# Value stage of a retrieval layer: 768 gathered and 1280 dense columns, and one weight split per two blocks

## The reference, cut to what matters

```python
def peer_layer(x, wq, keys, U, Vt):
    ...
    idx = jnp.take_along_axis(...)                       # 128 experts of 16384 for each token
    gate = jax.nn.softmax(best, axis=-1).astype(x.dtype)
    def blk(args):
        xb, ib, gb = args
        u = U[ib]
        hid = jax.nn.gelu(jnp.einsum('td,thkd->thk', xb, u))
        v = Vt[ib]
        return jnp.einsum('thk,thkd->td', gb * hid, v)   # the value stage
...
x = x + peer_layer(h2, ...)
return rms_norm(x, norm_f_g)
```

## Time and profile before

| | |
|---|---|
| median of 3 runs | 1992.54 us |
| the profiled execution | 1993.4 us |
| its span in the profile | 1991.7 us |
| value stage, first to last v_lo | 1504.37 to 1974.63 us |
| busy in the span: PE, DVE, ACT, POOL | 70%, 81%, 44%, 51% |
| TensorE's granted clock in the value stage | 1.00 (2.4 GHz) |

### The profile page before, as it was taken

The page is one execution under the profiler, slowest core; times in us unless marked ns, Lnnn a source line. Parts: engine busy times, 40 slices in busy tenths (PEclk is TensorE's granted clock), DMA queues, the critical chain, the costliest instruction groups (busy, mean ns, idle before and its releaser), DMA issues.

```text
span 1991.7 us, 22500 instructions
## 1 busy us (share of the span) xinstructions
PE 1401.3 (70%) x7813; PEld 1229.1 (62%) x7813; DVE 1614.4 (81%) x2065; ACT 875.9 (44%) x1279; POOL 1009.1 (51%) x705
## 2 busy tenths in 40 slices
PE   6999999999999999900000002221369999999997
PEld 6988998888888889900000001121257888888886
DVE  6466785556755566899999999987988999999998
ACT  4354443454444444322222235577754444444444
POOL 4002320000000003488888888888888768887772
PEclk9999999999999999955555555555579999999999
DMA  6555444545655555999999999999957999999996
GB/s 213 187 187 196 153 165 145 167 165 172 207 190 182 200 185 184 365 419 414 420 417 419 410 400 419 422 414 418 417 196 283 400 374 398 400 404 392 377 381 230
DMA packets 145660, 601.81 MB, mean 302 GB/s; under 512 B 14720, under 2 KB 14736, under 8 KB 110096
## 3 DMA queue, kind: packets, MB, share of 16 engines
q0 software_dynamic: 58048, 364.41, 45.2%
q1 hardware_dynamic: 87504, 236.02, 33.7%
HBM read 598.29 MB, written 2.10 MB: 301 GB/s over the span
## 4 chain that ended last, share of the span: by engine, by line
PE 61%; issue 14%; DVE 11%; POOL 6%; DMA 6%; ACT 1%; SPq 0%; DVEq 0%; POOLq 0%; ACTq 0%
PE acc L1956 8%; PE acc L1957 8%; PE acc L1958 8%; DVE slots L1632 6%; POOL slots L614 6%; PE acc L1937 5%; PE acc L1939 5%; PE acc L1940 5%; PE acc L2268 3%; PE acc L2269 3%; PE acc L2270 3%; PE scr L2269 3%; PE scr L2268 3%; PE scr L2270 3%; DMA slots<-in_peer_u,expert 3%
## 5 line engine op out<-in xcount | busy, mean ns | idle before, releaser
L1088 DVE TENSOR_TENSOR w_lo<-raw,w_hi 128x1024 fp32r<-128x1024 f32 x266 | 328.8, 1259 | 204.1 <-ACT w_hi L698 201.2
L1632 DVE SCALAR_TENSOR_TENSOR slots<-slots,acc 128x2048 f32<-128x2048 f32 x184 | 415.5, 2285 | 34.8 <-DMA slots<-in_peer_u,expert 32.8
L698 ACT ACTIVATE w_hi<-raw 128x1024 fp32r<-128x1024 f32 x272 | 281.9, 1056 | 360.3 <-PE acc L1958 176.4
L650 POOL DMA_INDIRECT starts<-in_v_gather,expert x256 | 357.8, 1398 | 102.8 <-DVE X L1856 73.0
L614 POOL DMA_INDIRECT slots<-in_peer_u,expert x256 | 257.8, 1007 | 100.2 <-issue 59.0
L624 POOL TENSOR_TENSOR slots<-slots,N 128x2048 f32<-128x2048 f32 x61 | 276.1, 4527 | 34.0 <-DMA slots<-in_peer_u,expert 33.9
L1022 ACT ACTIVATE v_hi<-v_raw 128x1344 fp32r<-128x1344 f32 x128 | 170.5, 1332 | 262.4 <-PE scr L2270 182.6
L938 ACT ACTIVATE slots<-slots 128x2048 f32<-128x2048 f32 x61 | 116.5, 1910 | 334.1 <-POOL slots L624 334.1
L2225 PE MATMUL scr<-hot_a,hot_b 128*128 128x128 f32 x448 | 89.0, 369 | 220.6 <-DVE hot_b L1709 158.3
L1856 DVE SCALAR_TENSOR_TENSOR X<-starts,weight,X 128x704 f32<-128x704 f32 x256 | 242.1, 946 | 1.4 <-issue 0.9
L1956 PE MATMUL acc<-w_hi,hT_hi 128*128 128x512 f32 x576 | 225.7, 392 | 0.6 <-DVE w_lo L1088 0.6
(11 more groups left out here) (329 smaller groups left out, 3079.6 us busy)
## 6 DMA issues: line engine op xcount, KB each, us to landing
raw<-in_w_in SPq DMA_DIRECT2D x88, 1024.0 KB
v_raw<-in_v_dense SPq DMA_DIRECT2D x128, 672.0 KB
raw<-in_w_o SPq DMA_DIRECT2D x16, 1024.0 KB
raw<-in_peer_wq SPq DMA_DIRECT2D x16, 1024.0 KB
raw<-in_w_a_up SPq DMA_DIRECT2D x8, 1024.0 KB
raw<-in_w_b_up SPq DMA_DIRECT2D x8, 1024.0 KB
slots<-in_peer_u,expert POOLq DMA_INDIRECT x256, 8.9
starts<-in_v_gather,expert POOLq DMA_INDIRECT x256
```

Of the source, the lines that this page charges most:

```text
L650: pool.indirect_dma_start(starts[j][:, :], None, v_gather[:, :], bass.IndirectOffsetOnAxis(ap=expert[:, s // NSEL, s % NSEL:s % NSEL + 1], ...
L698: a.activation(w_hi[:, m % 2, k, :], raw[:, m % 2, k, :], ACT.Copy).then_inc(hi_ready, 1)
L1088: v.tensor_tensor(w_lo[:, m % 2, k, :], raw[:, m % 2, k, :], w_hi[:, m % 2, k, :].bitcast(fp32), ALU.subtract).then_inc(lo_ready, 1)
L1632: v.scalar_tensor_tensor(out=slots[j][:, :], in0=slots[j][:, :], scalar=1.0, in1=row, op0=ALU.mult, op1=ALU.mult, accum_out=hid_sum[:, t, ...
```

## The change

CW goes from 704 to 768, so each gathered row is 64 columns wider and the dense part 64 columns narrower (1280; PE's third piece has 256 columns). The buffers of the value stage get new places in SBUF.

The weight splits of both tiles become one operation of 512 columns on ACT and one on DVE, in odd blocks only. For that the dense weights of both tiles are seen as rows of 8 KiB of one tensor, `weight_rows`, at the same addresses as before; `both_weights` takes one piece of two of its rows, the lower address first. Which of the two halves belongs to which tile is told by `side_of`.

```diff
-CW = 704
+CW = 768
...
 def weights_at(n):
     pair = (n + 1) // 2
-    return [(pair, 1 - n % 2)] if 0 < n and pair < BLOCKS // 2 else []
+    return [pair] if n % 2 and pair < BLOCKS // 2 else []
+
+def side_of(n, t):
+    return t if n < P // PIECES else 1 - t
...
+        def both_weights(pair):
+            q, at0 = 2 * pair // (P // PIECES), 2 * pair % (P // PIECES)
+            rows = sorted(((0, 14, 16, 19)[q] + at0 // 16, 2 + 2 * q + at0 // 16))
+            cols = slice(at0 % 16 * P, (at0 % 16 + 2) * P)
+            return weight_rows[:, rows[0]:rows[1] + 1:rows[1] - rows[0], cols]
...
-            def high_e(pair, t):
+            def high_e(pair):
                 if pair >= 2:
                     act.wait_ge(v_used, 4 * pair - 4)
-                q, at0 = 2 * pair // (P // PIECES), 2 * pair % (P // PIECES)
-                a.activation(e_hi[:, pair % 2, t, :],
-                             weight_of[t][q][:, at0:at0 + 2, :].rearrange("p a s -> p (a s)"), ACT.Copy
-                             ).then_inc(e_hi_ready, 1)
+                a.activation(e_hi[:, pair % 2, :, :], both_weights(pair), ACT.Copy).then_inc(e_hi_ready, 1)
...
-            def low_e(pair, t):
-                dve.wait_ge(e_hi_ready, 2 * pair + t + 1)
-                q, at0 = 2 * pair // (P // PIECES), 2 * pair % (P // PIECES)
-                v.tensor_tensor(e_lo[:, pair % 2, t, :],
-                                weight_of[t][q][:, at0:at0 + 2, :].rearrange("p a s -> p (a s)"),
-                                e_hi[:, pair % 2, t, :].bitcast(fp32), ALU.subtract).then_inc(e_ready, 1)
+            def low_e(pair):
+                dve.wait_ge(e_hi_ready, pair + 1)
+                v.tensor_tensor(e_lo[:, pair % 2, :, :], both_weights(pair), e_hi[:, pair % 2, :, :].bitcast(fp32),
+                                ALU.subtract).then_inc(e_ready, 2)
...
                 if n == 0:
-                    low_e(0, 0)
-                    low_e(0, 1)
+                    low_e(0)
                 add_start(2 * n)
-                for pair, t in weights_at(n):
-                    low_e(pair, t)
+                for pair in weights_at(n):
+                    low_e(pair)
                 add_start(2 * n + 1)
...
-                    pe.wait_ge(e_ready, n // 2 * 2 + t + 1)
+                    pe.wait_ge(e_ready, n // 2 * 2 + 2)
```

More of the change, by code:

```diff
@@ L310, in build @@
         masks_t = at("masks_t", 144, [MASKED, P])
-        weight_of1 = at("weight_of1", 32, [P, P])
-        weight_of = [[at(f"weight_of0_{q}", kib, [P // PIECES, P]) for q, kib in enumerate((16, 128, 144, 168))],
+        weight_rows = at("weight_rows", 16, [21, 16 * P])
+        weight_of1 = weight_rows[:, 2:10, :].rearrange("p r (a s) -> p (r a) s", s=P)
+        weight_of = [[weight_rows[:, r:r + 2, :].rearrange("p r (a s) -> p (r a) s", s=P) for r in (0, 14, 16, 19)],
                      [weight_of1[:, q * P // PIECES:(q + 1) * P // PIECES, :] for q in range(PIECES)]]
-        v_raw = [at(f"v_raw{n}", kib, [DW]) for n, kib in enumerate((112, 117.25, 2.75))]
+        def both_weights(pair):
[3 more added lines that the diff above has]
+            return weight_rows[:, rows[0]:rows[1] + 1:rows[1] - rows[0], cols]
+        v_raw = [at(f"v_raw{n}", kib, [DW]) for n, kib in enumerate((112, 117, 3))]
         v_hi = at("v_hi", 184, [2, DW], f32r)
-        v_lo = [at(f"v_lo{n}", kib, [DW], f32r) for n, kib in enumerate((160, 10.75))]
+        v_lo = [at(f"v_lo{n}", kib, [DW], f32r) for n, kib in enumerate((160, 11))]
         e_hi, e_lo = at("e_hi", 97, [2, NT, 2 * P], f32r), at("e_lo", 101, [2, NT, 2 * P], f32r)
@@ L321, in build @@
         y_first = at("y_first", 128, [NT, CW])
-        y_dense = at("y_dense", 133.5, [NT, DW])
+        y_dense = at("y_dense", 134, [NT, DW])
         starts = [at(f"starts{n}", kib, [CW]) for n, kib in enumerate(
-            (194.5, 197.25, 122.5, 125.25, 165.25, 105, 107.75, 24, 26.75, 29.5, 32.25, 35, 37.75, 40.5))]
+            (194, 197, 122, 125, 165, 105, 108, 24, 27, 30, 33, 36, 39, 42))]
         ff_room = at("ff_room", 200, [2 * KB])
@@ L1041, in square_first @@
                              ).then_inc(squared, 1)
-            high_e(0, 0)
-            high_e(0, 1)
+            high_e(0)
             for n in range(BLOCKS):
@@ L1047, in _ @@
                     high_v(n)
-                for pair, t in weights_at(n):
-                    high_e(pair, t)
+                for pair in weights_at(n):
+                    high_e(pair)
                 if n == FIRST_FROM:
@@ L2260, in add @@
                 def add(t, pieces, low):
-                    pe.wait_ge(e_ready, n // 2 * 2 + t + 1)
+                    pe.wait_ge(e_ready, n // 2 * 2 + 2)
                     flat = (acc, scr)[t][:, :, :].rearrange("p a n -> p (a n)")
-                    eh, el = e_hi[:, n // 2 % 2, t, e_cols], e_lo[:, n // 2 % 2, t, e_cols]
+                    eh, el = e_hi[:, n // 2 % 2, side_of(n, t), e_cols], e_lo[:, n // 2 % 2, side_of(n, t), e_cols]
                     for at0, end in pieces:
```

## The result

The changed kernel takes 1997.03 us (median of 16 runs, 1992.29 to 2001.60), the kernel before, run beside it, 1990.86 us (16 runs, 1987.39 to 1995.50). The ratio is 1.0030, 95% interval 1.0022 to 1.0037: slower by 6.2 us on the medians, where +7.3 was forecast. The profiled execution took 1996.16 us, with a span of 1994.4. Its value stage, from the first v_lo at 1503.73 to the last at 1977.60, is 473.9 us long against 470.3 before: +3.6 in these two executions.

The account below looks back on a forecast made before the run. PE bounds the value stage before the change at 3.64 us a block, DVE after it at 3.665. 465.9 undisturbed plus 11.7 late is 477.6 against 470.3, +7.3 on 1992.54: 1999.8 us, range 1991.2 to 2007.5.

Parts of the forecast that it names:

- DVE becomes the bound, alternating: Value stage: DVE sets the step, 3.46 us in even and 3.87 in odd blocks, mean 3.665, above PE's 3.48.
- The price of the dependence: In even blocks the second addition waits for the first, both writing X: 0.20 us that the split used to hide.
- 1.13 + 0.93: Part of DVE's even block of 3.46 us: 1.13 between the two additions' starts, then 0.93 to the next v_lo.
- Late loads: Dense loads landing late for v_hi in the value stage: 11.7 us forecast, between 0 and 20, against 7.5 before.
- 12 x 0.35: Growth in late loads: some 12 events, each with some 0.35 us less room, added to 7.5 for 11.7 us.
- rival 1: Value stage: late loads hidden, PE having 0.18 us a block to spare; with 3 us late, 1991.2 us; chance 0.28.
- the forecast's 8.4 to 16: Main case for the value stage: DVE the bound, with 8.4 to 16 us of lateness; chance 0.50.
- The sum: Value stage 465.9 us undisturbed plus 11.7 late, 477.6 against 470.3: +7.3 us, the run 1999.8 us.
- POOL: "waits for DVE's additions, as now": POOL in the value stage: as many gathers as before, waiting for DVE's additions as before; no size given.
- Rivals 2 and 3: 2: dependence costs DVE nothing, even block 3.26, 1987.3 us, chance 0.06; 3: DMA bounds, 2003.3 us, 0.16 with lateness above 16.

Follow-up runs that it names:

- two_tiles: The changed kernel with additions alternating between the two tiles, and tile 0's square and gain moved to the end: 2010.73 us, ratio 1.0103 to the kernel before.
- half_rows: The changed kernel with gathered rows of half the length (384 columns), each read twice by the addition: 1990.94 us, ratio 0.9998 to the kernel before.

## Why the prediction was right

- *DVE becomes the bound, alternating.* Right. Forecast 3.46 and 3.87, measured 3.52 and 3.86; PE's side waits 26.6 + 3.8 us on v_lo, against 8.0 + 3.7 before, where some 23 against 3.7 was forecast; the split takes 0.679 us (0.69).
- *The price of the dependence.* Forecast 0.20, from the pairs of the earlier trace rows. The runs show 2.13 - 1.94 = 0.19 without gathers, and 2.19 - 1.94 = 0.25 with them. The step that was mis-sized is "1.13 + 0.93", which took the pair of the earlier trace rows to the new width by the slope of DVE alone. That gives about what the pair takes without POOL (2.15 forecast, 2.13 measured); at the new width POOL's next issue starts 0.09 us into the second addition, which then takes 1.08 in place of 1.02, and 63 x 0.06 = 3.8 us were missed (the odd blocks, 0.01 shorter than forecast, give 0.6 back). So undisturbed the stage is 469.0, not 465.9. The rule of the Trainium skill in VectorE: DVE Perf Modes, The DRAIN you can't avoid, by which the wait would cost nothing, disagrees with two_tiles: 1.94 against 2.13 for the same two additions.
- *Late loads.* Forecast 11.7, from "12 x 0.35" on top of before's 7.5; measured 4.9. Of that, DVE idled 1.7 us ahead of a late v_lo (2.4 in its row, 0.7 of it before the first block) and some 2.4 for gathers (2.7 in their row, 0.3 of it the dependence), and the gain multiplication took 0.9; five pairs shorter than 2.19 give 0.4 back. So some 2 us is loads. This step failed: v_hi did wait for loads more often, 65 times for 147.2 us against 36 times for 77.5, but few of these waits reached DVE. The count was misread too: the 36 waits do not come in threes, in the trace they stand in 21 groups, most of them of one or two blocks. And the prediction counted each event of waits on ACT as lost time on DVE, with no cover behind it. But ACT starts v_hi as soon as the load is there, and since DVE itself is the bound, v_hi was mostly ready before DVE came to it (v_hi after such a wait runs from 1565.81 to 1567.09, and v_lo starts at 1567.54). To that extent rival 1 was right: 4.9 us lies in its range, below 8.4, and not in the forecast's 8.4 to 16. Whether the loads themselves landed later at 2.3% more bytes is not shown.
- *The sum.* The two errors, +3.1 undisturbed and -6.8 late, partly cancel (-3.7 on the stage): 473.9 against 477.6 for the stage in the profiled execution, which is +3.6 where +7.3 was forecast. On the medians it is +6.2 against +7.3, and that they are so close is in part luck: undisturbed the stage grew by 469.0 - 462.7 = 6.3 where 3.2 was forecast, and lateness, for which 4.2 more was forecast, did not grow in the two traced executions (7.6 and 4.9).
- *POOL: "waits for DVE's additions, as now".* The answer held for the time, but it wasn't priced. POOL's issues filled 354.2 us of the stage before and fill 382.0 now, with at least 0.30 between each two; the next thing that makes DVE faster at this width, two_tiles, ran into them at once.
- *Rivals 2 and 3* fall by two_tiles and half_rows.

## What to carry to other kernels

Removing an instruction that stands between two dependent ones can cost more than the instruction did: price the gap it filled, on the engine that will be the bound after the change, and look at what the other engines start at the moment in which the second of the two comes due. Two changes to one stage must be priced together, since the first may move the bound onto what the second lengthens. An engine's wait counts only as far as the engine that sets the step waits too.

## What the runs showed of the hardware that was not expected

POOL's issue of an indirect transfer of 128 rows takes longer beside a busy DVE, and can draw an instruction of DVE out in turn. It takes 0.94 to 2.96 us beside a busy DVE, a mean of 1630 ns in two_tiles; while DVE idles there for lack of a gather, from 1519.79 to 1522.16, it takes 0.94 or 0.95:

```profile
1521.23 0.94 POOL L663 DMA_INDIRECT starts<-in_v_gather,expert  x1 [0.30 <-issue]
```

Half the bytes (1629) and another kind of operation for v_lo (1609) change little. In the other direction an addition of 1.02 us into which such an issue starts 0.09 or 0.10 us behind its start takes 1.08 or 1.09 in 55 of 58 pairs, and in the three others the issue is drawn out instead. That most issues end 0.9 us after a start on DVE was read from the rows, not tried by itself.

The Trainium skill, SBUF — State Buffer, section SBUF: two separate sides, says that VectorE, with two inputs in SBUF, and GpSimd reading SBUF hold a pair of ports by turns, each for a whole instruction. That the two hold each other by turns agrees with these runs. That the one blocks the other for the whole instruction does not show here: an issue of 0.94 and an addition of 1.09 run side by side (1566.62 and 1566.53), and the addition is 0.07 us longer than the one of 1573.91. No run here shows the ports themselves.

The value stage ran at 386 GB/s on one core, and 40 us of it at 408. An earlier stage of the changed kernel ran at 415 for 500 us (900 to 1400), so the 406 that the prediction and the expectations name as the fastest is not the most that the DMA can bring.
